# Weighing and summing of the 32 gathered cache lines, spread over the whole attention loop by the keys of its units

## The chip, the cores and the metric

One NeuronCore of a Trainium2 chip runs the whole step as one program. The metric is the device time of one execution in microseconds (us). Three runs of the kernel before gave 2342.09, 2346.89 and 2352.07 us; their median is 2346.89 us. The profiled execution, from which all durations below come, took 2347.29 us.

## What is computed

The reference is one layer of a decoder. A prompt of 1024 tokens and 8 decode samples (one token each, with a past of 4096 positions) pass an input projection, three-branch attention (compressed, selected, window) beside a diagonal state-space model, an output projection, cross-attention and a SwiGLU feed-forward net. The part that the change touches is the compressed branch of the 8 samples. Their past lies in pages of 128 rows; each block of 32 rows is weighed with a table and summed, then projected:

```
def compress_blocks(rows, cmp_pos, cmp_proj):
    B, N = rows.shape[:2]
    blk = rows.reshape(B, N // CMP_BLOCK, CMP_BLOCK, 2, N_KV, HEAD_DIM)
    summ = jnp.einsum('bnlcgd,cld->bncgd', blk, cmp_pos)
    return jnp.einsum('bncgd,cde->bncge', summ, cmp_proj)
```

A softmax over those 128 compressed blocks of each sample then ranks the blocks of 64 rows; 13 of them (and the first and last) are fetched for the selected branch.

## The kernel before, in words

Everything stands in one hand-ordered program for five engines: PE (TensorE), DVE (VectorE), ACT (ScalarE), POOL (GpSimd) and SP (SyncE). All work tiles of PE pass through four PSUM slots in one written order, `psum_plan` (L136): a tile opens its slot when the tile four places earlier has been read out.

**The attention loop** (386 to 861 us of the span) handles the prompt. `attention_units` (L81) lists 136 units: 8 query tiles of 128 rows, for each first one compressed unit for all heads, then for each of 8 heads a selected unit with 128(i+1) keys and a window unit with at most 640 keys. In iteration a, PE computes the scores SC of unit a, the transposes TR of unit a-2 and the product with the values PV of unit a-3. DVE adds the bias to the scores and takes the row maximum (L2202, L2206), later scales the product into the output (L2233 for each head unit). ACT computes the exponential between the two, and copies the transposes out of PSUM. So SC of a unit goes PE, DVE, ACT, back to PE for TR, ACT for the copy, PE for PV, DVE for the output, with two iterations of lead (`AHEAD`).

**The lines.** The past rows of the samples come by indirect gathers as 32 "lines" (4 for each sample, `n` = line, `k = n // 8` is the quarter of the block, `b = n % 8` the sample), each 128 partitions by 2048 numbers. POOL gathers line n+1 into a ring of three tiles (`past_line`, L1270, `gring`) once line n-2 has been summed, and loads the table `posB` of a new quarter when the last line of the old one is weighed (`weigh_line`, L1277). DVE works on a line in three parts, one part at the end of an iteration (`sum_lines`, L2076): part 0 weighs all 2048 numbers (L2084), part 1 adds 1024 numbers to 1024, part 2 adds 512, then 256, and in quarters 1 to 3 adds 256 more to the running sum `summ`. The first part stands in iteration `SUMS_AT` = 2, and from then on there is one in every iteration, so the 96 parts fill iterations 2 to 97:

```
SUMS_AT = 2
BETWEEN = {SUMS_AT + 3 * 4 * DB + 1 + 2 * b: [("sT", b), ("sP", b)] for b in range(DB)}
BETWEEN.update({122: ["sc"], 124: ["sps", "scT"], 127: ["sov", "ix1"], 130: ["ix2"]})
```

**What stands between.** `BETWEEN` (L96) inserts the rest of the samples' compressed branch behind iterations: for each sample PE transposes its sums (`sT`), waits until ACT has copied them to `sTm` (L1527), and multiplies them with the projection (`sP`, L826 to 831), in iterations 99, 101, ..., 113. In iteration 122 the scores `sc` follow, in 124 `sps` and `scT` (with the selection chain on DVE, three operations over 960 numbers among others), in 127 `sov` and `ix1`, in 130 `ix2`, which gives DVE the line numbers of the selected rows (L2139). `sTm` are two buffers at 4128 of the arena, which is the place of the second ring tile.

**Behind the loop.** POOL waits for the line numbers, issues three gathers of selected rows (`gather`, L1319), waits until the last scores have been read, and issues 24 loads of the window rows `nbuf` (L1338 to L1342) into the place of the bias table. SP streams weights (`glu_w`, then eight tiles of `xkv`) from the end of the scores on, ACT loads `mem_prompt`. PE runs the gated unit's tiles, the memory keys and values `mk`, and then the window rows `wT` and the selected rows `gT`.

Of the kernel before, what the change touches and what calls it, by code (L numbers as in the profile page):

```python
# [16 lines left out]
P = 128  # L17
# [4 lines left out]
DB = 8  # L22
# [58 lines left out]
def attention_units():  # L81

    out = []
    for i in range(NT):
        out.append((i, 0, 0, 0, 4 * (i + 1)))
        for h in range(NH):
            out.append((i, h, 1, 0, P * (i + 1)))
            k0 = max(0, i - 4) * P
            out.append((i, h, 2, k0, P * (i + 1) - k0))
    return out  # L90
# [1 line left out]

SUMS_AT = 2
BETWEEN = {SUMS_AT + 3 * 4 * DB + 1 + 2 * b: [("sT", b), ("sP", b)] for b in range(DB)}  # L96
BETWEEN.update({122: ["sc"], 124: ["sps", "scT"], 127: ["sov", "ix1"], 130: ["ix2"]})

def ffn_items():  # L100
# [88 lines left out]
def hymba_step(nc, x_prompt, x_sample, cache_kv_cmp, cache_kv_sel, cache_kv_win, state_ssm_re, state_ssm_im,  # L189
# [8 lines left out]
    with ctx:  # L198
# [8 lines left out]
        flip = sb("flip", [P, P])  # L207
# [14 lines left out]
        pblk = sb("pblk", [P, 2, P])  # L222
# [3 lines left out]
        apow = sb("apow", [P, 6, 2, NPAIR])  # L226
# [14 lines left out]
        def at(first, *shape):  # L241
            n = int(np.prod(shape))
            v = A[:, first:first + n]
            if len(shape) == 2:
                v = v.rearrange("p (a b) -> p a b", b=shape[1])
            elif len(shape) == 3:
                v = v.rearrange("p (a b c) -> p a b c", b=shape[1], c=shape[2])
            elif len(shape) == 4:
                v = v.rearrange("p (a b c d) -> p a b c d", b=shape[1], c=shape[2], d=shape[3])
            return v  # L250
# [38 lines left out]
        CP = at(37152, 2, NPAIR, 5, 32)  # L289
        Tm = [at(42272, P), at(43296, P)]  # L290
        Wm = [at(42400, 2, P), at(43424, 2, P)]
        sTm = [at(4128, 2, P), at(4384, 2, P)]
        posB = at(43872, ROWS, P)
        WT = at(44896, 2, NPAIR, P)

# [97 lines left out]
        def slot(key):  # L393
            s = U[key] % 4
            return PS[:, 2 * s:2 * s + 2, :].rearrange("p a b -> p (a b)")
# [11 lines left out]
        filled = sem("filled")  # L407
# [94 lines left out]
        def full(eng, key):  # L502

            eng.wait_ge(filled, U[key] + 1)
# [5 lines left out]
        def free(ins, key):  # L510

            ins.then_inc(emptied[U[key] % 4], 1)
# [128 lines left out]
        def _(pe):  # L641
# [8 lines left out]
            def mm(out, lhsT, rhs, start=True, stop=True):  # L650
                return nc.tensor.matmul(out, lhsT=lhsT, rhs=rhs, start=start, stop=stop, skip_group_check=True)  # L651
# [41 lines left out]
            s = open_("par")  # L693
# [27 lines left out]
            s = open_("C")  # L721
# [3 lines left out]
            s = open_("h0")  # L725
            for part in range(2):
                for j in range(NPAIR):
                    c = (part * NPAIR + j) * DB
# [22 lines left out]
            for j in range(NPAIR):  # L751
# [3 lines left out]
                s = open_(("SB", j))  # L755
# [8 lines left out]
            for i in range(NT + 1):  # L764
                c0, n = token_tile(i)
                s = open_(("kv", i))
# [8 lines left out]
            s = open_("cproj")  # L775
# [7 lines left out]
            for j in range(NPAIR):  # L783
                s = open_(("V", j))
# [4 lines left out]
                if j >= 8:  # L789
                    h = j - 8  # L790
                    pe.wait_ge(hank_in[h % 2], 16 * (h // 2 + 1))
                    s = open_(("bt", h))
# [4 lines left out]
            s = open_("ys")  # L797
# [7 lines left out]
            s = open_("st")  # L805
            tr(s[0:32, 0:P], H[:, NC].rearrange("p a j -> p (a j)")).then_inc(filled, 1)
            for q in range(4):
                s = open_(("sst", q))
# [6 lines left out]
            def compressed_branch(key):  # L815

                if key[0] == "sT":

                    b = key[1]
                    pe.wait_ge(summ_ready, b + 1)  # L820
                    s = open_(key)
                    for c in range(2):
                        ins = tr(s[:, c * P:(c + 1) * P], summ[:, b, c * P:(c + 1) * P])
                    ins.then_inc(filled, 1)
                elif key[0] == "sP":

                    b = key[1]
                    read_out(pe, ("sT", b))
                    s = open_(key)
                    mm(s[:, 0:P], pblk[:, 0], sTm[b % 2][:, 0])  # L830
                    mm(s[:, P:2 * P], sTm[b % 2][:, 1], pblk[:, 1]).then_inc(filled, 1)
                elif key == "sc":

                    read_out(pe, ("sP", DB - 1))
                    read_out(pe, ("sP", DB - 2))
                    pe.wait_ge(qz_ready, 1)
                    s = open_(key)
                    for b in range(DB):
                        ins = mm(s[0:64, 0:P], qz[:, b], kcTs[:, b], b == 0, b == DB - 1)
                    ins.then_inc(filled, 1)  # L840
                elif key == "sps":

                    pe.wait_ge(pc_ready, 1)
                    s = open_(key)
                    mm(s[0:64, 0:P], same[:, :], Pc[0:64]).then_inc(filled, 1)
                elif key == "scT":
                    s = open_(key)
                    tr(s[:, 0:64], Pc[0:64]).then_inc(filled, 1)
                elif key == "sov":
                    read_out(pe, "scT")  # L850
                    s = open_(key)
                    for b in range(DB):
                        ins = mm(s[:, b * 8:b * 8 + 8], vcs[:, b], PcT[:, b * 8:b * 8 + 8])
                    ins.then_inc(filled, 1)
                elif key == "ix1":

                    pe.wait_ge(phys_ready, 1)
                    s = open_(key)
                    tr(s[0:SLOTS, 0:64], phys[0:64, 0:SLOTS]).then_inc(filled, 1)
                elif key == "ix2":  # L860
                    read_out(pe, "ix1")
                    s = open_(key)
                    mm(s[0:SL, 0:64], spread[:, :], p15[0:SLOTS]).then_inc(filled, 1)
# [4 lines left out]
            for a in range(n_at + AHEAD + 1):  # L868
                if a < n_at:
                    i, h, br, k0, nk = AT[a]  # L870
                    lo = 64 * (h % 2)
                    s = open_(("SC", a))
# [510 lines left out]
        def _(act):  # L1383
# [3 lines left out]
            def f(out, in_, func=ACT.Copy, **kw):  # L1387
                return a_.activation(out, in_, func, **kw)  # L1388
# [132 lines left out]
            def compressed_branch(key):  # L1521
                if key[0] == "sT":
                    b = key[1]
                    full(act, key)
                    if b >= 2:
                        full(act, ("sP", b - 2))
                    free(f(sTm[b % 2].rearrange("p a c -> p (a c)"), slot(key)[:, 0:256]), key)  # L1527
                elif key[0] == "sP":
                    b = key[1]
                    full(act, key)  # L1530
                    own.step(f(kcTs[:, b], slot(key)[:, 0:P]))
                    free(f(vcs[:, b], slot(key)[:, P:2 * P]), key)
                elif key == "sps":
                    softmax_rows(1, pw_raw, pw_exp, Pc[0:64], 64)
                elif key == "scT":
                    full(act, key)
                    free(f(PcT, slot(key)[:, 0:64]), key)
                elif key == "sov":
                    full(act, key)
                    free(f(osT[:, 0], slot(key)[:, 0:64]), key)  # L1540
                elif key == "ix1":
                    full(act, key)
                    free(f(p15[0:SLOTS], slot(key)[0:SLOTS, 0:64]), key)
# [232 lines left out]
        def _(dve):  # L1776
# [299 lines left out]
            def sum_lines(n, part):  # L2076

                k, b = n // DB, n % DB
                flat = gring[n % 3]
                if part == 0:  # L2080
                    dve.wait_ge(gat[n % 3], 16 * (n // 3 + 1))
                    dve.wait_ge(posB_in, 32 * (k + 1))
                    r = flat.rearrange("p (r c g d) -> p (r c) g d", r=ROWS, c=2, g=2)
                    tt(r, r, posB.rearrange("p r (c d) -> p (r c) d", c=2).unsqueeze(2)  # L2084
                       .to_broadcast([P, 2 * ROWS, NKV, HD])).then_inc(weighted, 1)
                elif part == 1:
                    dve.wait_ge(weighted, n + 1)
                    own.step(tt(flat[:, 0:1024], flat[:, 0:1024], flat[:, 1024:2048], ALU.add))
                else:
                    own.settle()  # L2090
                    own.then(tt(flat[:, 0:512], flat[:, 0:512], flat[:, 512:1024], ALU.add))
                    if k == 0:
                        tt(summ[:, b], flat[:, 0:256], flat[:, 256:512], ALU.add).then_inc(gat_used, 1)
                    else:
                        own.then(tt(flat[:, 0:256], flat[:, 0:256], flat[:, 256:512], ALU.add))
                        tt(summ[:, b], summ[:, b], flat[:, 0:256], ALU.add).then_inc(gat_used, 1)
                    if k == 3:
                        dve.wait_ge(gat_used, n + 1)
                        dve.sem_inc(summ_ready, 1)
# [57 lines left out]
            for a in range(n_at + AHEAD + 1):  # L2157
# [76 lines left out]
                if t + 1 >= 0 and t + 1 < n_at:  # L2234
# [7 lines left out]
                    else:  # L2242
                        tt(st[:, 56 + rn:57 + rn], st[:, 48 + rn:49 + rn], gates[:, i, 3 * h + br:3 * h + br + 1])\
                            .then_inc(dve_gate, 1)
                if 0 <= a - SUMS_AT < 3 * 4 * DB:
                    sum_lines((a - SUMS_AT) // 3, (a - SUMS_AT) % 3)
                for key in BETWEEN.get(a, []):
                    compressed_branch(key)

# [266 lines left out]
```

## Time and profile before

| | |
|---|---|
| median of three runs | 2346.89 us |
| profiled execution | 2347.29 us |
| its span on the core | 2345.6 us |
| attention loop in it | 385.9 to about 861 us |
| busy PE / DVE / ACT over the span | 86% / 44% / 26% |
| granted TensorE clock, mean of the execution | 0.879 of full |

A time outside the span (2347.29 - 2345.6 = 1.7 us) is start and end of the program and is not touched. Busy shares are averages over stages with different limits, so the loop is read query tile by query tile.
### The profile page before, as it was taken

To read this page: it belongs to the slowest core of one execution; us is meant where nothing else is said; L and a number is where in the kernel's file an instruction comes from. 1 tells how busy PE (TensorE), PEld (TensorE's weight loads), DVE (VectorE), ACT (ScalarE), POOL (GpSimd) and SP (SyncE) were. 2 spreads that over 40 slices of the span, in tenths; PEclk is the share of its full clock that TensorE was granted. 3 is DMA by queue.
4 is the path that set the end of the run, shared out by engine and by line. 5 is a ranking of instruction groups with operands and counts; after the bars stand their busy time and mean duration, and the time that the engine had idled before them with its cause. 6 is when DMAs were issued, how large, how long until landed. Compare 5 with 4: busy or idle time off the path is not lost.

```text
span 2345.6 us, 28566 instructions
## 1 busy us (share of the span) xinstructions
PE 2026.3 (86%) x11440; PEld 1735.8 (74%) x11440; DVE 1038.6 (44%) x2439; ACT 609.3 (26%) x1228; POOL 140.3 (6%) x236
## 2 busy tenths in 40 slices
PE   7699997788888988676978899589999999999994
PEld 5465554577777877544975586489999999999993
DVE  6859725999884531005243031623232322323235
ACT  3031113334445441213232122521111111111112
POOL 2001112101100020200000100000000000000000
PEclk9899897557888899666998879789999999999997
DMA  5020003433310065730300301011111111111102
GB/s 127 20 73 32 32 0 119 143 118 121 114 55 1 1 160 179 167 88 10 118 28 27 135 1 36 28 39 52 37 55 37 52 48 48 52 37 55 37 19 81
DMA packets 122315, 151.19 MB, mean 64 GB/s; under 512 B 13256, under 2 KB 104560, under 8 KB 116136
## 3 DMA queue, kind: packets, MB, share of 16 engines
q0 software_dynamic: 17152, 80.63, 11.2%
q1 hardware_dynamic: 102600, 60.77, 9.0%
q10 hardware_dynamic: 2432, 7.96, 0.9%
q8 instruction: 92, 1.51, 0.3%
q14 instruction: 39, 0.32, 0.0%
HBM read 137.03 MB, written 12.31 MB: 64 GB/s over the span
## 4 chain that ended last, share of the span: by engine, by line
PE 48%; DVE 5%; issue 2%; DMA 1%; ACT 1%; POOL 0%; DVEq 0%; POOLq 0%
PE PS L651 46%; PE PS L655 2%; DVE A L2372 1%; DVE A L1781 1%; ACT A L1388 1%; DMA A<-in_cache_mem_kv 1%; DMA A<-new_selected_row 0%; DVE hL L1781 0%; DVE hRaw L1781 0%; DVE A L2383 0%; DVE A L2346 0%; DMA A<-in_norm_g 0%; DVE mA L1781 0%; DVE mS L2348 0%; DVE A L2324 0%
## 5 line engine op out<-in xcount | busy, mean ns | idle before, releaser
L651 PE MATMUL PS<-A 128*128 128x64 f32 (+15 forms) x3728 | 747.9, 361 | 35.5 <-ACT A L1388 28.0
L651 PEld LDWEIGHTS PS<-A 128*128 128x128 f32 (+4 forms) x3728 | 554.2, 206 | 227.2 <-issue 72.8
L655 PE MATMUL PS<-ident,A 128*128 128x128 f32 (+7 forms) x1528 | 277.3, 331 | 207.8 <-DVE A L2383 53.8
L655 PEld LDWEIGHTS PS<-ident,A 128*128 128x128 f32 (+7 forms) x1528 | 211.3, 166 | 257.9 <-issue 61.2
L1388 ACT ACTIVATE A<-PS 128x256 f32<-128x256 f32 (+17 forms) x404 | 229.0, 586 | 607.1 <-PE PS L651 487.0
L1781 DVE TENSOR_TENSOR A<-A 128x1024 f32<-128x1024 f32 (+12 forms) x397 | 304.6, 773 | 9.5 <-DMA A<-in_cmp_pos 0.3
L651 PE MATMUL PS<-hH,wL 128*128 128x344 f32 x1056 | 224.2, 321 | 2.9 <-issue 2.9
L651 PE MATMUL PS<-hL,wH 128*128 128x344 f32 x1056 | 224.3, 321 | 0.0
L651 PE MATMUL PS<-hH,wH 128*128 128x344 f32 x1056 | 223.7, 320 | 0.0
L651 PEld LDWEIGHTS PS<-hH,wL 128*128 128x128 f32 x1056 | 177.2, 189 | 4.1 <-issue 4.1
L651 PEld LDWEIGHTS PS<-hL,wH 128*128 128x128 f32 x1056 | 177.7, 189 | 0.0
L651 PEld LDWEIGHTS PS<-hH,wH 128*128 128x128 f32 x1056 | 177.3, 188 | 0.0
L1781 DVE TENSOR_TENSOR wL<-wRaw,wH 128x1024 fp32r<-128x1024 f32 (+2 forms) x76 | 82.1, 1082 | 208.1 <-ACT wH L1388 207.9
L1388 ACT ACTIVATE A<-A,st 128x640 f32<-128x640 f32 (+9 forms) x131 | 96.4, 736 | 248.5 <-DVE st L2206 225.1
L1388 ACT ACTIVATE wH<-wRaw 128x1024 fp32r<-128x1024 f32 (+2 forms) x76 | 71.6, 944 | 213.4 <-PE PS L651 213.4
L1781 DVE TENSOR_TENSOR A<-A,PS 128x688 f32<-128x688 f32 x112 | 72.4, 688 | 117.2 <-PE PS L651 113.9
L651 PE MATMUL PS<-gH,wL 128*128 128x344 f32 x528 | 114.2, 325 | 8.6 <-DVE A L1781 4.1
L651 PE MATMUL PS<-gL,wH 128*128 128x344 f32 x528 | 112.5, 321 | 0.0
L651 PE MATMUL PS<-gH,wH 128*128 128x344 f32 x528 | 112.2, 321 | 0.0
L1781 DVE TENSOR_TENSOR gRaw<-gRaw,PS 128x688 f32<-128x688 f32 (+1 forms) x44 | 28.5, 688 | 183.1 <-PE PS L651 183.1
L651 PE MATMUL PS<-kL,qS 128*128 128x512 f32 (+3 forms) x192 | 89.1, 464 | 12.3 <-DVE qS L1781 12.3
L651 PEld LDWEIGHTS PS<-gH,wL 128*128 128x128 f32 x528 | 87.6, 189 | 15.1 <-issue 15.1
(266 smaller groups left out, 1778.3 us busy)
## 6 DMA issues: line engine op xcount, KB each, us to landing
wRaw<-in_ffn_wi SPq DMA_DIRECT2D x44, 512.0 KB, 3.7
wRaw<-in_ffn_wo SPq DMA_DIRECT2D x28, 384.0 KB, 3.0
out<-A POOLq DMA_DIRECT2D x16, 512.0 KB, 3.2
A<-in_cache_mem_kv POOLq DMA_DIRECT2D x16, 512.0 KB, 5.3
A<-in_x_prompt SPq DMA_DIRECT2D x8, 512.0 KB, 8.1
A<-in_w_in SPq DMA_DIRECT2D x8, 512.0 KB, 10.6
A<-bias_by_distance POOLq DMA_DIRECT2D x8, 512.0 KB, 3.9
A<-in_xkv SPq DMA_DIRECT2D x8, 512.0 KB, 12.5
```

The source lines that it names most:

```text
L651: return nc.tensor.matmul(out, lhsT=lhsT, rhs=rhs, start=start, stop=stop, skip_group_check=True)
L655: return nc.tensor.transpose(out, in_, ident[b:b + n, b:b + n])
L1388: return a_.activation(out, in_, func, **kw)
L1781: return v.tensor_tensor(out, a, b, op)
L2372: free(v.scalar_tensor_tensor(dtmp[0:r, i % 2], slot(key)[0:r], st[0:r, 9 + i % 2:10 + i % 2], grow[0:r], ALU.mult, ALU.mult), key)
```

## The change

`line_starts` gives each unit a cost of 1000 plus its keys, and starts a line wherever 1/32 of the cost of units 2 to 125 has gone by (at least three iterations apart). Worked out, the starts are iterations 2, 8, 13, 18, 22, 27, 32, 36, 40, 45, 49, 53, 57, 61, 64, 68, 72, 76, 79, 83, 86, 90, 93, 97, 100, 104, 107, 110, 113, 117, 120 and 123; a line's three parts stand in three iterations in a row. `sT` and `sP` of a sample move to the iteration behind its last part: 103, 107, 110, 113, 116, 120, 123, 126. `sc` moves from 122 to 131, `sps` and `scT` from 124 to 133, `sov` and `ix1` from 127 to 135, `ix2` from 130 to 137. Since the ring is now in use while `sT` runs, `sTm` moves to `flip` and the first part of `apow` (both free by then), is one buffer for each half instead of two for both, and ACT copies it in two pieces.

```
-SUMS_AT = 2
-BETWEEN = {SUMS_AT + 3 * 4 * DB + 1 + 2 * b: [("sT", b), ("sP", b)] for b in range(DB)}
-BETWEEN.update({122: ["sc"], 124: ["sps", "scT"], 127: ["sov", "ix1"], 130: ["ix2"]})
+def line_starts():
+
+
+    cost = [1000 + nk for _, _, _, _, nk in attention_units()]
+    total, gone, starts = sum(cost[2:126]), 0, []
+    for a in range(2, 126):
+        if len(starts) < 4 * DB and gone >= total * len(starts) / (4 * DB) and (not starts or a >= starts[-1] + 3):
+            starts.append(a)
+        gone += cost[a]
+    return starts
+
+
+LINE_AT = line_starts()
+SUMS = {a + part: (n, part) for n, a in enumerate(LINE_AT) for part in range(3)}
+BETWEEN = {LINE_AT[3 * DB + b] + 3: [("sT", b), ("sP", b)] for b in range(DB)}
+BETWEEN.update({131: ["sc"], 133: ["sps", "scT"], 135: ["sov", "ix1"], 137: ["ix2"]})
...
-        sTm = [at(4128, 2, P), at(4384, 2, P)]
+        sTm = [flip[:, :], apow[:, 0:4].rearrange("p a b c -> p (a b c)")]
...
-                    mm(s[:, 0:P], pblk[:, 0], sTm[b % 2][:, 0])
-                    mm(s[:, P:2 * P], sTm[b % 2][:, 1], pblk[:, 1]).then_inc(filled, 1)
+                    mm(s[:, 0:P], pblk[:, 0], sTm[0])
+                    mm(s[:, P:2 * P], sTm[1], pblk[:, 1]).then_inc(filled, 1)
...
-                    if b >= 2:
-                        full(act, ("sP", b - 2))
-                    free(f(sTm[b % 2].rearrange("p a c -> p (a c)"), slot(key)[:, 0:256]), key)
+                    if b >= 1:
+                        full(act, ("sP", b - 1))
+                    own.step(f(sTm[0], slot(key)[:, 0:P]))
+                    free(f(sTm[1], slot(key)[:, P:2 * P]), key)
...
-                if 0 <= a - SUMS_AT < 3 * 4 * DB:
-                    sum_lines((a - SUMS_AT) // 3, (a - SUMS_AT) % 3)
+                if a in SUMS:
+                    sum_lines(*SUMS[a])
```

Counted by query tile (iterations 17i to 17i+16), the 96 parts stood 15, 17, 17, 17, 17, 13, 0, 0 before and stand 9, 11, 12, 13, 14, 15, 15, 7 after. Insertions of `sT` and `sP` stood 2 in tile 5 and 6 in tile 6, and stand 5 in tile 6 and 3 in tile 7.

## Rows read from the trace of the kernel before

**Rows 1.** The page's head: the span, and busy time of each engine.

```profile
span 2345.6 us, 28566 instructions
...
PE 2026.3 (86%) x11440; PEld 1735.8 (74%) x11440; DVE 1038.6 (44%) x2439; ACT 609.3 (26%) x1228; POOL 140.3 (6%) x236
```

**Rows 2.** Windows, one per query tile: length; busy PE, PEld, DVE, ACT, POOL; clock; DMA.

```profile
385.90:436.70 50.80, 27.44 (x115) 21.28 (x114) 34.44 (x122) 20.80 (x60) 10.48 (x19) 0.55 0.45 154
436.70:484.60 47.90, 38.53 (x163) 31.19 (x162) 42.88 (x141) 16.68 (x58) 7.71 (x8) 0.50 0.39 127
484.60:537.30 52.70, 46.25 (x211) 39.68 (x210) 46.98 (x149) 20.16 (x59) 6.89 (x8) 0.60 0.36 125
537.30:590.40 53.10, 43.38 (x259) 36.48 (x258) 49.34 (x143) 23.92 (x59) 5.43 (x6) 0.84 0.34 119
590.40:650.40 60.00, 51.50 (x339) 46.50 (x338) 53.32 (x158) 26.65 (x58) 7.71 (x8) 0.86 0.33 109
650.40:717.50 67.10, 59.51 (x378) 54.29 (x377) 51.05 (x161) 31.80 (x65) 1.92 (x2) 0.82 0.11 37
717.50:786.50 69.00, 59.64 (x428) 54.98 (x427) 30.15 (x128) 35.37 (x78) 0.00 (x0) 0.90 0.00 1
786.50:861.00 74.50, 69.56 (x503) 64.23 (x503) 39.82 (x169) 34.92 (x64) 11.56 (x20) 0.91 0.28 62
```

**Rows 3.** Waits of the stretch 406 to 650: total, times, longest.

```profile
ACT A L1388 <- DVE st L2206: 136.1, 76, 5.1
```

**Rows 4.** Groups by form, DVE, 386 to 720: the adds and weighing of the lines.

```profile
L1781 DVE TENSOR_TENSOR A<-A 128x2048 f32<-128x2048 f32 x32 | 73.1, 2285 | 0.3 <-DMA A<-in_cmp_pos 0.3
L1781 DVE TENSOR_TENSOR A<-A 128x1024 f32<-128x1024 f32 x32 | 39.0, 1219 | 0.0
...
L1781 DVE TENSOR_TENSOR A<-A 128x256 f32<-128x256 f32 x56 | 23.8, 425 | 1.9
L1781 DVE TENSOR_TENSOR A<-A 128x512 f32<-128x512 f32 x32 | 21.9, 685 | 0.0
```

**Rows 5.** Windows of L2233 alone (one for each head unit): length, busy DVE (count), clock.

```profile
651.30:700.70 49.40, 3.29 (x12) 0.83 0.13 44
777.80:796.20 18.40, 1.70 (x6) 1.00 0.00 1
723.50:777.80 54.30, 3.12 (x11) 0.87 0.00 1
800.40:842.50 42.10, 2.53 (x9) 0.84 0.04 10
842.60:855.70 13.10, 1.14 (x4) 1.00 0.99 210
```

**Rows 6.** Windows, all engines, of the first of those five stretches.

```profile
651.30:700.70 49.40, 43.18 (x273) 39.22 (x272) 42.02 (x124) 23.57 (x48) 1.92 (x2) 0.83 0.13 44
```

**Rows 7.** Windows, all engines, ten microseconds late in query tile 2.

```profile
526.00:536.00 10.00, 9.63 (x40) 8.33 (x40) 9.37 (x29) 4.16 (x13) 2.81 (x3) 0.50 0.46 147
```

**Rows 8.** Timeline around one insertion: start, length, engine, operation, idle before.

```profile
742.93 1.17 ACT L1388 ACTIVATE A<-PS 128x896 f32<-128x896 f32 x2
...
744.15 0.49 PE L651 MATMUL PS<-A,pblk 128*128 128x128 f32 x2 [1.39 <-ACT A L1388]
...
744.90 0.45 ACT L1388 ACTIVATE A<-PS 128x128 f32<-128x128 f32 x2 [0.80 <-PE PS L651]
```

**Rows 9.** Timeline of POOL: first selected gather, first load of the window rows.

```profile
839.00 1.00 POOL L1322 DMA_INDIRECT A<-in_cache_kv_sel,line  x1 [169.42 <-DVEq L2141]
...
854.15 0.57 POOL L1338 DMA_DIRECT2D A<-in_cache_kv_win  x1 [9.82 <-DVE st L2206]
```

**Rows 10.** Timeline of PE behind the loop: the one wait for weights.

```profile
901.79 16.18 PE L651 MATMUL PS<-A 128*128 128x128 f32 x128 [3.35 <-DMA A<-in_xkv]
```

**Rows 11.** Windows behind the loop, all engines, DMA share and GB/s last.

```profile
880.00:900.00 20.00, 17.08 (x141) 16.62 (x139) 8.55 (x24) 1.54 (x4) 4.25 (x8) 0.94 0.98 308
900.00:920.00 20.00, 18.21 (x148) 18.09 (x148) 0.00 (x0) 2.58 (x7) 0.00 (x0) 0.91 0.49 139
```

## The prediction

> **What bounds the kernel now.** The page comes first: the profiled execution has a span of 2345.6 us, and PE is busy for 86% of it [rows 1]. That share says little about one stage, so the next view is the windows, cut at the loop's eight query tiles. The whole loop is 475 us. In tile 0 DVE is busy 34.4 of 50.8 us; the loop only starts to run some 20 us into it. In tiles 1 to 4 DVE is busy 42.88 of 47.9, 46.98 of 52.7, 49.34 of 53.1 and 53.32 of 60.0 us, so 89 to 93%, while PE stands at 80 to 88%, mostly at a low granted clock (0.50, 0.60, 0.84, 0.86). In tile 6, which has no part of a line, DVE is busy 30.15 of 69.0 us [rows 2]. The waits say the same: from 406 to 650 us ACT stood 136.1 us, 76 times, for the scores' evacuation on DVE [rows 3]. So DVE paces tiles 1 to 4 and most of 5, and PE with its round trips over ACT paces 6 and 7. The change takes DVE work from the first group and gives it to the second.
>
> **What is moved.** By form, the weighing is 32 x 2285 ns, the first add 32 x 1219, the second 32 x 685 and the 256 adds 56 x 425: 73.1 + 39.0 + 21.9 + 23.8 = 157.8 us, over 96 parts 1.64 us each, and 1.54 in quarter 0, which has one add less [rows 4]. Nothing of it goes away. The parts by tile go from 15, 17, 17, 17, 17, 13, 0, 0 to 9, 11, 12, 13, 14, 15, 15, 7, so the question is what a part costs where it leaves and where it lands.
>
> **Where parts leave.** Tile 0 loses 6: at most 6 x 1.54 = 9.2 us. Its PE ran at a clock of 0.55 and there are short units without cover behind it, so I take -6 (ends -3 and -9.2). Tile 1 loses 6: DVE would need 9.9 us less, 38.0 us at the same idleness, but PE is busy 38.53 us at 0.50 [rows 2], so PE at its lower level stops it near 40.5: -7 (ends -5 and -9.9). Tile 2 loses 5, 8.2 us at most. Late in it PE at 0.50 is busy 9.63 of 10 us [rows 7], so at the lower level almost nothing could be gained, while at the tile's mean clock of 0.60 PE has 6.5 us of idle time: -7 (ends -1 and -8.2). Tile 3 loses 4: -6.5 (at most 6.6), as its clock of 0.84 leaves PE 9.7 us idle. Tile 4 loses 3: -4.5 (at most 4.9). For the clock of these tiles the rows show 0.50 while PE waited in every unit for DVE, and 0.84 to 0.86 from tile 3 on, where units are longer.
>
> The Trainium skill, page "TensorE: Matmul & The Clock Gate", section "What's actually happening", says that the throttled state is the default and that activity releases it. By that rule a PE that DVE holds up less would be granted its upper level sooner, and tiles 0 to 2 would give all of 9.2 + 9.9 + 8.2 us in place of 20, so 7 us more; no stretch of this trace shows tile 1 at the upper level.
>
> **Tiles 5 to 7.** The unit is the price here. L2233 runs once for each head unit. With a part in every iteration, 13 units of tile 5 (12 and a compressed one) took 49.4 us, 3.80 each; 6 units of tile 6 without part or insertion took 18.4 us, 3.07 each; 12 units of tile 6 (11 and a compressed one) with 6 insertions of sT and sP took 54.3 us, so an insertion costs (54.3 - 12 x 3.07) / 6 = 2.9 us; 9 units of tile 7 across sc, sps, sov, ix1 and ix2 took 42.1 us, and 4 bare ones 13.1 us, 3.27 each, so that chain costs 42.1 - 29.4 = 12.7 us [rows 5]. Check: 17 x 3.07 + 6 x 2.9 = 69.6 for tile 6, against 69.0 in the windows. In those 13 units DVE was busy 42.0 of 49.4 us [rows 6]; it is the bound there, with the usual gaps of its fences. A part in a late iteration therefore costs 3.80 - 3.07 = 0.73 us, not 1.64: the rest runs while DVE would wait for PE. Its ends are 0 (all covered) and 1.64 (nothing covered).
>
> An insertion costs because sT needs an ACT copy that stands behind an exponential and a long copy in ACT's order: PE idles before sP, and SC of the next unit is queued behind it, with DVE and then ACT waiting for that [rows 8]. After the change five of the eight insertions (107, 110, 113, 120, 123) share their iteration with a part 0, whose 2.29 us run on DVE meanwhile. I take 2.3 us for each (ends 0.6, that is 2.9 - 2.29, and 2.9). The extra copy piece on ACT is cheap: two 128x128 copies together take 0.45 us [rows 8], so at most 0.2 x 8 = 1.6 us, inside these ends. The single buffer's wait for the sP before it is for one at least three iterations old: nothing. The new operands (flip, apow) are read like the old ones: nothing.
>
> Tile 5: 15 x 3.80 + 2 x 3.07 = 63.1, before 67.1: -4. Tile 6: 63.1 + 5 x 2.3 = 74.6, before 69.0: +5.6. Tile 7: 7 parts x 0.73 = 5.1, 3 insertions x 2.3 = 6.9, and the chain from sc to ix2 now lies in the last eight iterations, three of which have no scores, so some of its 12.7 us falls together with the emptying of the pipeline: -2 (ends 0 and -6). Together +10.
>
> **Queues moved past.** POOL's gathers of lines follow the sums by themselves; it waits for DVE before each of them, so they merely come later. The line numbers of the selected rows were ready at 839, 22 us before the loop's end, and the window rows' loads began at 854.2 [rows 9]. Now ix2 stands in the last iteration but one. The three gathers (120 rows of 8 KB each, 2.95 MB; 1 us each on POOL, and a small load behind each) start with the loop's end at 861, so the 24 loads begin near 866 in place of 854, 12 us later. PE reads the window rows only after mk, which ends at 918 [rows 10], so nobody waits for those directly. But the DMA engines stood at a share of 0.98 and 308 GB/s from 880 to 900 and at 0.49 after that [rows 11], while the xkv weights came in, and PE waited once for them, 3.35 us [rows 10]. 2.95 MB at 308 GB/s are 9.6 us of traffic more in that stretch. With half of the next 20 us free I take +3 (ends -4, since mem_prompt and the first weights meet fewer window rows, and +9.6).
>
> **The sum.** Leaving: -6 -7 -7 -6.5 -4.5 -4 = -35. Arriving: +5.6 + 10 + 3 = +18.6. Net -16.4: 2347.3 - 16.4 = 2331 us. The profiled execution stands 0.4 us over the median of the runs, so the forecast for the median is the same, 0.7% faster. Its own range is 2322 to 2342. A measurement of this kernel can tell about 0.5% (12 us) from no change: below 2335 is faster, above 2359 slower.
>
> **The rivals.**
> A, chance 0.20: late parts are covered. In tile 6 DVE idles 39 of 69 us [rows 2], and two iterations of lead could absorb a part. Then tiles 6 and 7 change only by the insertions, -2.9 + 8.7 - 2 = +3.8, and the sum is -35 + 3.8 + 3 = -28: 2319, and 2312 with the 7 us of the early clock. The rule of the clock gate named above is part of this case. Against it: the 3.80 us units of tile 5 exist.
> B, chance 0.26: no difference. Either tiles 1 and 2 stay at the lower level and PE stops them early (-22 in place of -35), or DMA traffic behind the loop costs its 9.6 us and an insertion its full 2.9 us (8 x 0.6 more). The first gives -22 + 18.6 = -3, the second -16.4 + 6.6 + 4.8 = -5: about 2343. For it: PE at 0.50 was 96% busy in places.
> C, chance 0.06: slower. The mechanism is the order on DVE: a part stands between the output of one unit and the evacuation of the next scores, and SC of the unit after waits for the slot. If PE meets that gap in each late iteration, a part costs its full 1.64 us: tile 6 becomes 69.0 + 15 x 1.64 - 2.9 = 90.7 (+21.7), tile 7 +7 x 1.64 + 8.7 = +20.2, together +41.9 and with 9.6 behind the loop +51.5 against -35: +16, 2364. It decides from the price p of a late part: with full insertions and +3 behind the loop the sum is -35 - 2.9 + 8.7 + 3 + 22p, which is zero at p = 1.2 us. Against it: 13 units of tile 5 show 3.80, not 3.07 + 1.64 = 4.71.
> That the change doesn't move what it says can be left out: the starts follow from the code.
>
> **How the numbers follow.** Forecast 0.48, A 0.20, B 0.26, C 0.06. Of the forecast's own share 0.42 lies below 2335. Faster 0.42 + 0.20 = 0.62, same 0.06 + 0.26 = 0.32, slower 0.06. The range takes in the forecast's ends, most of A and of B: 2314 to 2350.
>
> **What would show it.** Windows of the changed kernel by query tile: DVE's load near 0.9 in tiles 2 to 6; lengths near 45, 41, 46, 46.5, 55.5, 63, 74.5 and 84.5 us. Tile 6 longer than 69 us confirms the price of late parts; 66 or less speaks for A, 85 or more for C. PE's clock in tiles 1 and 2: over 0.7 means that the early clock rose. The gap of PE before each sP shows the insertions. PE's wait for xkv behind the loop should lie between 3 and 10 us. The prediction is wrong if tiles 0 to 4 give less than 20 us together, or tiles 6 and 7 take more than 30.

## The result, and the profile after

The changed kernel took 2363.05 us (median of four runs, 2362.05 to 2371.06) against 2347.47 us before: a ratio of 1.008, with a 95% interval of 1.0053 to 1.0107. The forecast was 2331 us with a range of 2314 to 2350. The kernel became slower by 16 us, 0.8%, where 0.7% faster was forecast.

The profiled execution is the slowest of the four, 2371.06 us, so 8 us over their median; a second profiled execution of the same kernel took 2364.11 us. Where the two differ, both are given. The page's head, which answers to [rows 1]:

```profile
span 2369.3 us, 28575 instructions
...
PE 2051.2 (87%) x11440; PEld 1762.1 (74%) x11440; DVE 1038.1 (44%) x2439; ACT 609.0 (26%) x1236; POOL 139.9 (6%) x236
```

The windows of the changed kernel by query tile answer to [rows 2] (length; busy PE, PEld, DVE, ACT, POOL; granted clock; DMA share; GB/s):

```profile
383.60:430.70 47.10, 25.72 (x115) 20.90 (x114) 27.25 (x116) 20.65 (x60) 8.55 (x17) 0.54 0.36 122
430.70:472.90 42.20, 37.26 (x163) 31.39 (x162) 31.92 (x127) 16.55 (x58) 3.73 (x4) 0.50 0.30 100
472.90:519.90 47.00, 43.60 (x209) 37.71 (x208) 39.07 (x134) 20.15 (x58) 5.77 (x6) 0.61 0.32 102
519.90:573.50 53.60, 45.90 (x259) 39.21 (x258) 44.90 (x144) 23.55 (x58) 4.14 (x5) 0.77 0.23 79
573.50:629.60 56.10, 49.07 (x339) 44.92 (x338) 47.50 (x151) 27.00 (x58) 6.27 (x7) 0.88 0.32 104
629.60:699.30 69.70, 60.84 (x368) 56.21 (x367) 52.35 (x159) 29.40 (x59) 6.63 (x7) 0.78 0.25 84
699.30:777.60 78.30, 65.19 (x422) 59.70 (x421) 52.56 (x152) 34.30 (x78) 4.85 (x5) 0.83 0.20 68
777.60:877.50 99.90, 87.54 (x520) 79.67 (x520) 52.27 (x188) 38.60 (x78) 1.57 (x2) 0.75 0.06 17
```

DVE carries what the change says: 42.88 us of tile 1 became 31.92, and the 30.15 of tile 6 became 52.56. Lengths in us; the last column is the span less the end of the loop, which is read here at 860.7 for the kernel before ([rows 2] cut it at 861.0):

| | tile 0 | 1 | 2 | 3 | 4 | 5 | 6 | 7 | behind the loop |
|---|---|---|---|---|---|---|---|---|---|
| before | 50.8 | 47.9 | 52.7 | 53.1 | 60.0 | 67.1 | 69.0 | 74.2 | 1484.9 |
| after, first profile | 47.1 | 42.2 | 47.0 | 53.6 | 56.1 | 69.7 | 78.3 | 99.9 | 1491.8 |
| after, second profile | 46.2 | 42.2 | 48.8 | 53.9 | 56.6 | 63.7 | 75.7 | 96.4 | 1492.2 |
| mean change | -4.2 | -5.7 | -4.8 | +0.6 | -3.7 | -0.4 | +8.0 | +23.9 | +7.1 |
| forecast | -6 | -7 | -7 | -6.5 | -4.5 | -4 | +5.6 | +10 | +3 |

So three things went wrong at once: tiles 0 to 4 gave 18 us in place of 31 (and tile 5 nothing in place of 4), tile 7 took 24 in place of 10, and the stretch behind the loop 7 in place of 3. The timeline of the changed kernel shows what happens at the end of tile 7 (start, length, engine, operation, idle time before it):

```profile
851.92 1.15 DVE L1795 TENSOR_TENSOR A<-A,jota 64x960 f32<-64x960 f32 x1
...
853.19 1.15 DVE L1795 TENSOR_TENSOR A<-A 64x960 f32<-64x960 f32 x1
...
854.38 1.15 DVE L2150 TENSOR_REDUCE A<-A 64x15 f32<-64x960 f32 x1
...
856.87 1.30 PE L668 MATMUL PS<-ident,A 128*128 128x128 f32 x5 [3.33 <-DVE st L2220]
...
859.05 6.97 PE L664 MATMUL PS<-A 128*128 128x64 f32 x32 [0.88 <-ACT A L1401]
...
875.81 0.99 POOL L1335 DMA_INDIRECT A<-in_cache_kv_sel,line  x1 [108.03 <-DVEq L2155]
```

The three operations over 960 numbers hold DVE while the scores of the last unit but one wait for it; PE waits 3.33 us for their evacuation. By then no further scores are left for PE to work on in the meantime. The windows before and after that wait:

```profile
838.30:856.70 18.40, 13.83 (x104) 12.24 (x103) 11.51 (x48) 5.27 (x12) 0.00 (x0) 0.97 0.10 30
856.70:875.80 19.10, 18.05 (x83) 17.33 (x83) 3.25 (x22) 5.70 (x10) 0.00 (x0) 0.50 0.19 55
```

PE ran at a granted clock of 0.97 before the wait and at 0.50, its lower level, for 19 us after it, 18.05 of them busy, with the 16 small products of `sov` (8 columns each) and the last transposes and products of the loop. The first gather is issued at 875.8, with the loop's end at 877.5.

The second profile shows that this one wait is not the whole story. There PE has no such wait, but it is at its lower level already 8 us earlier, counted from the end of the loop, behind a wait of 1.00 us for the samples' softmax:

```profile
841.58 0.69 PE L664 MATMUL PS<-A,same 64*64 64x128 f32 x2 [1.00 <-DVE A L2088]
```

The same two products took 0.43 us in the first profile. Yet from the start of `sc` to the end of the loop the two executions took nearly the same: 38.0 us (839.50 to 877.5) and 38.3 us (831.92 to 870.2). Behind the loop PE waits for the norm of `mem_prompt` (6.86 us, 4.42 before) and twice for weights of `xkv` (once, 3.35 us, in [rows 10]):

```profile
899.23 3.67 PE L668 MATMUL PS<-ident,A 128*128 128x128 f32 x16 [6.86 <-DVE A L2269]
...
920.56 16.04 PE L664 MATMUL PS<-A 128*128 128x128 f32 x128 [5.33 <-DMA A<-in_xkv]
937.59 3.84 PE L664 MATMUL PS<-A 128*128 128x128 f32 x32 [0.98 <-DMA A<-in_xkv]
```

### The profile page after: what moved, and what is told of

Same layout as the page of the kernel before. It is cut to its first block, busy times and chain, and to the rows that moved or that the text cites. A ratio compares the mean times of both kernels' runs of the same rounds, so it can differ in the third digit from the quotient of the medians.

```text
span 2369.3 us, 28575 instructions
## 1 busy us (share of the span) xinstructions
PE 2051.2 (87%) x11440; PEld 1762.1 (74%) x11440; DVE 1038.1 (44%) x2439; ACT 609.0 (26%) x1236; POOL 139.9 (6%) x236
## 4 chain that ended last, share of the span: by engine, by line
PE 47%; DVE 5%; issue 2%; DMA 1%; ACT 1%; POOL 0%; DVEq 0%; POOLq 0%; ACTq 0%
PE PS L664 45%; PE PS L668 2%; DVE A L2386 1%; DVE A L1795 1%; ACT A L1401 1%; DMA A<-in_cache_mem_kv 1%; DMA A<-new_selected_row 1%; DVE hL L1795 0%; DVE hRaw L1795 0%; DVE A L2360 0%; DVE A L2397 0%; DVE mA L1795 0%; DMA A<-in_norm_g 0%; DVE mS L2362 0%; DVE A L2338 0%
## 5 line engine op out<-in xcount | busy, mean ns | idle before, releaser
L664 PE MATMUL PS<-A 128*128 128x64 f32 (+15 forms) x3728 | 760.7, 366 | 37.6 <-ACT A L1401 27.1
L664 PEld LDWEIGHTS PS<-A 128*128 128x128 f32 (+4 forms) x3728 | 568.2, 211 | 226.8 <-issue 72.0
L668 PE MATMUL PS<-ident,A 128*128 128x128 f32 (+8 forms) x1528 | 288.5, 341 | 201.4 <-DVE A L2397 50.2
L668 PEld LDWEIGHTS PS<-ident,A 128*128 128x128 f32 (+8 forms) x1528 | 221.4, 172 | 251.9 <-issue 56.7
L1401 ACT ACTIVATE A<-PS 128x1024 f32<-128x1024 f32 (+16 forms) x396 | 226.4, 590 | 612.0 <-PE PS L664 491.2
L1401 ACT ACTIVATE A<-A,st 128x640 f32<-128x640 f32 (+9 forms) x131 | 96.4, 736 | 260.6 <-DVE st L2220 236.7
```

The lines of the kernel that those rows point to most:

```text
L668: return nc.tensor.transpose(out, in_, ident[b:b + n, b:b + n])
```

## The experiments

They ran in three groups, each beside the kernel before on one chip; its median in the groups was 2346.8, 2345.9 and 2347.1 us. Times of different groups, such as the changed kernel (2363.05 and 2362.7) and most of its variants, are therefore comparable to about 1 us on top of their own scatter. Theory 1, formed from the profile above: the parts of the lines are about neutral, and it is the tail (sc to ix2 in the last eight iterations) that costs. The rival: parts in the late iterations cost it.

**The changed kernel again.**

> The changed kernel once more, for a second profile of it. Its first profile was 8 us above its other runs. If the stretches at the lower clock level in query tiles 3 and 5 are a feature of the schedule, both tiles come out as before (53.6 and 69.7 us, within 1 us); if they are chance, they differ by several us. Time: 2363.

2362.7 us (ratio 1.006, 1.0043 to 1.0077). Tile 5 took 63.7 us at a clock of 0.84, against 69.7 at 0.78; tile 3 stayed at 53.9. So 6 us of the first profile's 8 were chance in tile 5, and tile 3's missing gain is a feature of the schedule. Later runs bear it out: tiles 0 to 4 have the program of the kernel before in four other runs below and that of the changed kernel in three, so there are five profiles of each. The means of tiles 0 to 4 are 50.6, 47.8, 53.1, 53.3 and 58.7 us before and 46.4, 41.9, 47.3, 53.1 and 56.8 us after, 263.4 and 245.5 together: 18 us, and nothing in tile 3.

**Only insertions and tail late.**

```
-LINE_AT = line_starts()
+LINE_AT = [2 + 3 * n for n in range(4 * DB)]
```

with the positions of `BETWEEN` written out as in the change.

> The lines' parts stand in iterations 2 to 97 as in the kernel before; only sT and sP (103 to 126) and sc to ix2 (131 to 137) stand where the change puts them, and sTm too. Theory 1, that the late chain is what costs (PE waits for DVE's selection chain with no scores left to cover it, falls to the lower clock, and the gathers start with the loop's end): 12 to 20 us slower than before, 2359 to 2367. Rival, that the parts in the late iterations are what costs: 0 to 5 us over before, at most 2352.

2360.9 us, 1.0059 (1.0039 to 1.0079): 14 us slower, with not one part moved, as theory 1 has it. The changed kernel is only 2 us slower than this run, which the scatter of both covers: spreading the parts came out about neutral. The profiled execution is the fastest of the four, 2352.8 us, 8 us under their median, so its windows show less than the usual time. Tiles 6 and 7:

```profile
707.30:769.70 62.40, 54.74 (x422) 50.26 (x421) 30.46 (x131) 35.63 (x81) 0.00 (x0) 0.97 0.00 1
769.70:859.30 89.60, 81.79 (x520) 74.82 (x520) 39.62 (x169) 37.00 (x75) 1.58 (x2) 0.80 0.07 19
```

**Only the tail late.**

```
-BETWEEN.update({122: ["sc"], 124: ["sps", "scT"], 127: ["sov", "ix1"], 130: ["ix2"]})
+BETWEEN.update({131: ["sc"], 133: ["sps", "scT"], 135: ["sov", "ix1"], 137: ["ix2"]})
```

> The kernel before with nothing changed but the places of sc, sps and scT, sov and ix1, ix2: 131, 133, 135, 137 in place of 122, 124, 127, 130. The insertions stay at 99 to 113. Theory 1 (this tail is what costs, not the places of the insertions): 10 to 15 us slower than before, of which about 7 in query tile 7 and 7 behind the loop. Rival (the three insertions among the units of tile 7, or their meeting with the tail, cost it): within 5 us of before.

2360.5 us, 1.0056 (1.0032 to 1.008). This one line of the change costs 15 us; the two intervals don't part it from the whole change. Tiles 6 and 7:

```profile
716.40:786.30 69.90, 61.39 (x426) 56.58 (x425) 30.13 (x128) 35.27 (x78) 0.00 (x0) 0.88 0.00 1
786.30:866.80 80.50, 72.33 (x502) 66.85 (x502) 39.54 (x169) 34.94 (x64) 1.57 (x2) 0.88 0.08 21
```

Tile 7 is 6.3 us longer than before; behind the loop stand 1495.2 us (2362.0 - 866.8) in place of 1484.9, so 10.3 more (7.1 in the changed kernel; what makes the 3 us between them is open). Where the 6.3 come from shows when both tiles are cut at the first scores of the last selected unit but one, here and in the kernel before:

```profile
830.65 0.50 PE L651 MATMUL PS<-kL,qS 128*128 128x512 f32 x1
```

```profile
842.00 0.48 PE L651 MATMUL PS<-kL,qS 128*128 128x512 f32 x1
```

Up to there the tile takes 44.4 us in place of 55.5: moving the chain away gave 11.1. From there to the end of the loop it takes 36.2 us (830.65 to 866.8) in place of 18.7 (842.00 to 860.7): landing it at the end cost 17.5. Before, PE was at its upper level in that stretch (1.00 from 838.3 to 860.7); here it is at 0.55 from 845.0 to 866.8, behind a wait of 3.33 us like the one above. How the 17.5 us divide between waits and the lower level was not separated.

**Window rows first.** On POOL the three gathers go behind the 24 loads, in the changed kernel:

```
-            pool.wait_ge(line_ready, 1)
-            pool.wait_ge(gat_used, 4 * DB)
-            for n in range(3):
-                gather(n)
...
                 pool.dma_start(nbuf[P - 1:P, b, 3], win_row[b:b + 1]).then_inc(nbuf_in, 16)
+            pool.wait_ge(line_ready, 1)
+            pool.wait_ge(gat_used, 4 * DB)
+            for n in range(3):
+                gather(n)
```

> The changed kernel with POOL issuing the 24 loads of the window rows before it waits for the line numbers and issues the first three selected gathers. The stretch behind the loop was 7 us longer than before. If POOL's order, which starts the window rows 12 us later, is the cause, 5 to 7 us faster than the changed kernel. If the 2.95 MB of gathers in that stretch are the cause whatever the order, within 3 us of it.

2358.2 us, 1.0048 (1.0028 to 1.0068), 4.5 us under the changed kernel by the medians, though the ten times lie between 2347.9 and 2367.6 and the interval overlaps the changed kernel's. The profile is clearer than the times: behind the loop stand 2356.9 - 871.5 = 1485.4 us, as before the change, and the waits for `xkv` are gone:

```profile
892.75 3.68 PE L668 MATMUL PS<-ident,A 128*128 128x128 f32 x16 [6.24 <-DVE A L2268]
897.79 30.31 PE L664 MATMUL PS<-A 128*128 128x128 f32 x256 [1.36 <-issue]
```

The whole of `mk` (256 products) now runs in one piece of 30.3 us. The wait for the norm stays (6.24 us). The loads of the window rows now start at 852.8 and are all issued by 864.8, before the loop's end at 871.5; in the changed kernel they start at 881.1, behind its end at 877.5. The 2.95 MB of gathers start at the loop's end in both. So by these profiles, one against two, it was the order on POOL, which pushed the window rows among the weights, and not the gathers' own traffic, that cost 6 to 7 us.

**sP one iteration behind sT, before the change and after it.**

```
-BETWEEN = {LINE_AT[3 * DB + b] + 3: [("sT", b), ("sP", b)] for b in range(DB)}
+BETWEEN = {LINE_AT[3 * DB + b] + 3: [("sT", b)] for b in range(DB)}
+BETWEEN.update({LINE_AT[3 * DB + b] + 4: [("sP", b)] for b in range(DB)})
```

and the same in the kernel before, at 99 + 2b and 100 + 2b.

> The kernel before with sP one iteration behind its sT (sT in 99, 101, ..., 113, sP in 100, 102, ..., 114). Theory 1: an insertion costs 2.9 us because PE waits for ACT's copy of sT in the same iteration; with an iteration between, most of 8 x 2.9 = 23 us goes: 12 to 20 us faster, 2327 to 2335. Rival: ACT's copy stands behind the exponential in either case and the wait only moves to the next tile in that PSUM slot: within 4 us of before.

2335.2 us, 0.9955 (0.9935 to 0.9974). Tile 6 falls from 69.0 to 58.0 us and holds the upper level throughout:

```profile
708.60:766.60 58.00, 53.12 (x430) 49.83 (x429) 30.33 (x131) 35.52 (x80) 0.00 (x0) 1.00 0.00 1
766.60:842.60 76.00, 70.24 (x502) 64.70 (x502) 39.44 (x168) 34.97 (x64) 11.20 (x20) 0.89 0.27 61
```

> The changed kernel with each sP one iteration behind its sT. In the kernel before the same edit gave 11.6 us. If an insertion among late parts stalls in the same way, 10 to 16 us faster than the changed kernel, 2347 to 2353. If the parts on DVE had covered most of the stall already, as the prediction took it in part, at most 5 us.

2348.5 us, 1.0019 (0.9996 to 1.0041), so 14 us under the changed kernel. Tiles 6 and 7, which were 77 and 98 us in the mean of the two profiles:

```profile
693.40:761.50 68.10, 59.81 (x422) 54.77 (x421) 53.59 (x159) 34.82 (x79) 4.85 (x5) 0.90 0.24 83
761.50:853.10 91.60, 82.75 (x520) 75.05 (x520) 50.70 (x182) 37.51 (x78) 1.57 (x2) 0.81 0.06 18
```

The same edit gave 12 us before the change and 14 after it, alike within the scatter: late parts don't cover an insertion's stall. PE's waits for the copy of sT (total, times, longest) in tile 6 of the changed kernel are:

```profile
PE PS L664 <- ACT apow L1401: 10.1, 5, 3.0
```

and in tile 6 of the kernel with only the insertions and the tail late:

```profile
PE PS L664 <- ACT apow L1401: 5.9, 5, 1.9
```

Both have the same five insertions there. In the changed kernel each follows an iteration that ends with a part 2 on DVE, which could delay the next scores, ACT's exponential and, behind it, the copy PE waits for. That is not shown: in the next run four of the five insertions follow a lightened part, and the same waits still come to 9.6 us, against 10.1 here and 8.4 in the second profile of the changed kernel. A part 2 keeps its adds of 256 there, 0.85 us of 1.5, so the reading isn't refuted either; what makes the waits longer stays open.

**The late parts made light.** Lines 25 to 31 (iterations 104 to 125), with `few = n >= 25`:

```
+                    m = 1 if few else 2 * ROWS
+                    r = flat.rearrange("p (r c g d) -> p (r c) g d", r=ROWS, c=2, g=2)[:, 0:m]
...
+                    m = 16 if few else 1024
...
+                    m = 16 if few else 512
```

> The changed kernel, with the parts of the last seven lines (iterations 104 to 125) worked on few columns: part 0 on 128 of 2048, part 1 on 16 of 1024, part 2's first add on 16 of 512. Most of the weighing and summing of these lines is left out, some 24 us of DVE work. Prediction's price (0.73 of 1.64 us for a late part): 10 to 12 us faster than the changed kernel. Rival C (a late part costs all its time): 22 to 26 us faster. Rival A (covered): within 4 us.

2353.7 us, 1.0034 (1.0012 to 1.0055), 9 us under the changed kernel. Tiles 6 and 7:

```profile
696.10:771.60 75.50, 64.95 (x422) 60.38 (x421) 38.97 (x163) 35.56 (x81) 4.86 (x5) 0.82 0.21 73
771.60:866.00 94.40, 82.69 (x520) 76.11 (x520) 42.82 (x183) 37.74 (x77) 1.58 (x2) 0.79 0.06 18
```

DVE's load in these tiles fell by 23.0 us (52.56 + 52.27 to 38.97 + 42.82), so a us of late DVE work costs 9.2 / 23.0 = 0.40 us (9.2 from 2362.9, the mean of the changed kernel's two medians). The prediction had 0.73 / 1.64 = 0.45. The ten times of this run lie between 2345.5 and 2366.6 us, so by an estimate from that scatter the 9.2 are 3 to 13 and the price 0.1 to 0.6. That is under rival C's full price, and in accord with the prediction's; it hardly parts the prediction from rival A, which allowed 4 us.

**All parts made light, before and after the change.** The same edit for every line. The first run has the program of the kernel before with the light parts, the second that of the changed kernel.

> The kernel before with every part worked on few columns (part 0 on 128 of 2048, part 1 on 16 of 1024, part 2's first add on 16 of 512), so most of the weighing and summing is left out: about 110 us of DVE work less. It gives the floor of query tiles 0 to 5 without parts. The prediction has DVE as the bound of tiles 1 to 4 and PE at its lower level close under it in tiles 1 and 2: then tiles 1 and 2 stop near 40 us each, and tiles 3 and 4 fall to 40 and 50. Rival: tile 3 stays near 50 us, so what the change took from it could give nothing.

2282.1 us, 0.9703 (0.9663 to 0.9743). Tiles 0 to 5 of the first, the floor under the parts:

```profile
380.30:419.70 39.40, 24.68 (x115) 20.75 (x114) 18.15 (x124) 21.51 (x63) 10.49 (x19) 0.56 0.54 182
419.70:456.90 37.20, 36.12 (x163) 31.52 (x162) 23.84 (x140) 16.98 (x58) 7.63 (x8) 0.50 0.55 180
456.90:496.80 39.90, 33.26 (x211) 28.75 (x210) 27.19 (x144) 19.51 (x57) 7.38 (x8) 0.84 0.50 167
496.80:540.60 43.80, 39.11 (x258) 33.85 (x258) 29.17 (x142) 23.98 (x61) 4.91 (x6) 0.88 0.43 145
540.60:591.60 51.00, 47.18 (x337) 43.18 (x336) 34.51 (x160) 27.01 (x59) 7.69 (x8) 0.90 0.40 128
591.60:650.00 58.40, 53.74 (x380) 49.78 (x379) 35.13 (x158) 30.17 (x63) 1.91 (x2) 0.88 0.12 43
```

Tiles 1 to 4 fall to 37.2, 39.9, 43.8 and 51.0 us, about where the expectation had them (40, 40, 40 and 50), and tile 3 doesn't stay near 50. But the price of a us of DVE work is far from 1: 53.2 us for 94.1 us of work in tiles 0 to 4 together, 0.57, and in tile 3 alone 9.3 for 20.2, 0.46.

> The changed kernel with every part worked on the same few columns. If the late chain, and not the parts, is what makes the changed kernel slow, it stays 12 to 20 us behind the same edit of the kernel before. If the late parts are the cause, the two come out within 5 us of each other.

2291.2 us, 0.9755 (0.9719 to 0.9792), so 9 us behind, between the two expectations. Its tiles 1, 3 and 5:

```profile
423.90:457.30 33.40, 32.38 (x161) 29.35 (x160) 21.06 (x128) 17.08 (x61) 3.43 (x4) 0.55 0.37 126
...
494.90:536.00 41.10, 36.20 (x259) 30.60 (x258) 28.64 (x139) 22.43 (x57) 4.39 (x5) 0.96 0.31 104
...
581.50:632.20 50.70, 46.05 (x369) 42.34 (x367) 34.26 (x156) 29.14 (x59) 6.63 (x7) 1.00 0.33 108
```

Both edits take 111 us of DVE work away (1038.6 to 927.8 us busy over the span, and 1038.1 to 927.1). Before the change that gives 65 us, after it 72: 0.59 and 0.65 us of time for each us of DVE work. Spread over the loop, the parts cost in total no less than packed at its start, by the medians.

**Lines spread over a shorter stretch.** `range(2, 112)` in place of `range(2, 126)`, tail at 122 to 130 as before.

> The lines spread in proportion to the keys, but over iterations 2 to 112, sT and sP in 95... no: in 92, 95, ..., 113, and sc to ix2 at 122 to 130 as before. Parts by query tile 10, 13, 14, 15, 16, 17, 11, 0. Theory 1 (the late chain costs, the parts are worth about 1 us each where they leave and cost 0.73 us where they land): 0 to 8 us faster than before, about 2343. Rival (late parts cost their full 1.64 us): 15 parts land for 15 that leave, so 3 to 8 us slower.

2349.3 us, 1.0017 (1.0002 to 1.0032). 2.5 us slower than before: theory 1's 0 to 8 us faster is missed, and the rival's 3 to 8 us slower is met but for half a us. The rival's price, the full time of a late part, isn't shown by that, since the light late parts gave less. Tiles 0 to 2 gave what they give in the changed kernel (46.1, 41.9, 47.1 us), and tiles 5 and 6 took it back (77.0 and 74.4).

**Distance for every round trip, without and with the shorter spread.** The second half of the edit beyond sP:

```
+for _a, _keys in {119: ['sc'], 120: ['sx'], 121: ['sy'], 122: ['sps', 'scT'], 123: ['s1'], 124: ['s2', 'sov'], 125: ['s3'], 127: ['ix1'], 129: ['ix2']}.items():
+    BETWEEN.setdefault(_a, []).extend(_keys)
```

where `sx` is the exponential on ACT, `sy` the division on DVE, and `s1` to `s3` the three operations over 960 numbers.

> The kernel before with every round trip of the samples' branch given an iteration of its own: sP one behind sT; scores in 119, exponential on ACT in 120, the division on DVE in 121, sps and scT in 122, the three operations over 960 numbers in 123, 124 and 125, sov in 124, ix1 in 127, ix2 in 129. The 12.7 us that sc to ix2 cost are waits of PE for these round trips. If giving them distance takes the waits away, 18 to 24 us faster than before (11.6 for the insertions, the rest here): 2322 to 2328. If only the insertions give, 2335.

2331.2 us, 0.992 (0.9894 to 0.9946): the fastest run that does all the work, 16 us under the kernel before. It falls between the two expectations (2322 to 2328, and 2335), and its interval overlaps that of the split insertions alone. The profiled execution is its slowest, 2340.1 us. Tiles 6 and 7:

```profile
721.60:779.60 58.00, 53.11 (x430) 49.83 (x429) 30.32 (x131) 35.49 (x79) 0.00 (x0) 1.00 0.00 1
779.60:848.90 69.30, 66.22 (x502) 61.17 (x502) 39.07 (x169) 34.88 (x64) 11.23 (x20) 0.95 0.31 70
```

Tile 7 lost 5 us against 74.2 before, and 7 against 76.0 with only the insertions split. So of the 12.7 us that the expectation called waits, distance took away about half.

> The same round trips with distance, and the lines spread in proportion to the keys over iterations 2 to 112 in place of 2 to 97. Without the stalls of the insertions, PE keeps its upper level in tiles 5 and 6, and the parts that left tiles 0 to 2 show: 5 to 12 us faster than the kernel with the parts in 2 to 97, about 2316. Rival: what tiles 0 to 2 give is taken back in tiles 5 and 6, within 3 us of it.

2335.8 us, 0.9943 (0.9917 to 0.9968): 4.7 us slower than without the spread by the medians, within the scatter of both. The 5 to 12 us of gain didn't come; the rival's 3 us are passed a little, to the slow side. Tiles 5 and 6:

```profile
638.50:708.10 69.60, 61.38 (x387) 56.86 (x385) 55.44 (x164) 31.27 (x70) 7.70 (x8) 0.80 0.27 89
708.10:782.10 74.00, 65.66 (x419) 60.51 (x419) 49.05 (x152) 35.80 (x81) 0.94 (x1) 0.82 0.09 29
```

Tile 6 is 16 us longer than without the spread (58.0), at a clock of 0.82 in place of 1.00, for 11 parts and 18.7 us more of DVE work; tiles 0 to 2 gave 14.7 us (151.8 to 137.1 us together).

## Why the prediction was wrong

**What bounds the kernel now.** "DVE paces tiles 1 to 4" was half right. The busy share of 89 to 93% was read as a bound. With 65 us for 111 us of work, DVE was close to the bound but not alone on the path: 0.59 us of time for each us of its work.

**Where parts leave.** This is the first step that failed. The 24 parts that left tiles 0 to 4 took 36.3 us of DVE work with them (227.0 to 190.6 us busy), and the prediction credited -6 -7 -7 -6.5 -4.5 = -31 for them, 0.85 for each us. The two profiles show -17.8, so 0.49. A part was priced at nearly its full time where it left and at 0.45 of it where it landed; the runs show about half at either end, and with one price a move gives nothing. The changed kernel stands 2 us from the run with the parts left in place (2362.9 and 2360.9), and the spread to 112, with the tail in its old place, 2.5 us over the kernel before. The prediction had the ceiling of each tile in its own rows: [rows 5] gave 0.45 for the same work in tile 5, and nothing but the busy share said that tiles 1 to 4 were different. For tiles 0 to 2 the lower clock was named as the stop and -20 in total taken; -14.7 came. The largest miss is tile 3, -6.5 forecast: it gave nothing (+0.6) at a clock of 0.77 and 0.78 in place of 0.84, with 4.4 us less on DVE. With all parts light the same tile gave 9.3 us for 20.2, so it can give, but the first 4.4 us bought nothing. The clock alone doesn't explain it: in another profile of the same stretch, that of the changed kernel with split insertions, it was 0.84 again, and the tile still took 53.2 us. Why stays open. Tile 5 gave 0.4 in place of 4, and its five profiles run from 62.7 to 69.7 us.

**Tiles 5 to 7.** The price of a landing part isn't contradicted by the times (0.40, from 0.1 to 0.6, against 0.45), but single tiles show more: tile 6 with 15 parts took 77.0 us against 62.4 with none and the same insertions, for 22.7 us of DVE work, 0.64, and the spread to 112 with split insertions 16 us for 18.7. The insertion at 2.3 us was too cheap: three of them among tile 7's units, without parts, made it 89.6 in place of 80.5 us, 3.0 each, just over the upper end of 2.9. The idea that a part 0 in the same iteration would cover the stall was wrong: PE's waiting at an insertion was 1.2 us without parts and 2.0 with them (1.7 in the second profile).

**The tail.** The second step that failed, and the costliest: "-2 (ends 0 and -6)". It assumed that waits fall together with the emptying of the pipeline. The run with the tail alone late shows +6.3 in tile 7, outside both ends. The chain's price where it left was about right, 11.1 us against 12.7; where it landed it was 17.5 in place of the 10.7 that the sum assumes. The waits of sc to ix2 are followed by scores of later units before the change; at the end there are hardly any, and PE falls to its lower level, which the sum did not hold at all. Tile 7 as a whole can be followed from run to run: 74.2 before, 80.5 with the tail late, 89.6 with three insertions too, 98.1 with seven parts too. The steps of 6.3, 9.1 and 8.5 add up to the 23.9 by construction, and each rests on one or two profiles.

**Queues moved past.** The mechanism was named: gathers first, window rows 12 us later, PE waiting for `xkv`. The term was mis-sized, +3 in place of 7, which lies under its upper end of 9.6 (10.3 with the tail alone late). The window rows began 27 us later (881.1 in place of 854.2) and not 12, and the price was put on the gathers' traffic, where by the profile it was the window rows that met the weights.

**The rivals.** A (parts covered) is made unlikely by the 9 us that light late parts gave and by tile 6. C said slower, and slower it was, by 16 us, which is near C's 2364 by luck and not by C's mechanism: with the tail alone late and no part moved, about 15 of the 16 us are there. Of B the sizes came true, a gain of 18 where the parts left (it had 22), insertions at 3.0 us, 7 us behind the loop, all together where it took them one by one; but its reason was tiles 1 and 2 stopped early, and these missed by 3.5 us, tiles 3 and 5 by 10.7. What no rival held was that the tail itself costs 15 us. The conditions that it named for being wrong ("if tiles 0 to 4 give less than 20 us together, or tiles 6 and 7 take more than 30") came out on both counts: 17.8 and 31.9.

On the rule of the Trainium skill's page "TensorE: Matmul & The Clock Gate", section "What's actually happening": the tail agrees with it in the fall, 0.97 before the wait and 0.50 behind it, but not in what follows: PE was busy 18.05 of the next 19.1 us, and that activity didn't release the lower level. The hope drawn from it, that PE would rise to its upper level sooner in tiles 0 to 2, was not met: 0.54, 0.50 and 0.61 after against 0.55, 0.50 and 0.60 before, although PE was less held up. Even with hardly any part left, tile 1 stayed at 0.50 with PE busy 36.12 of 37.2 us.

## What to carry to other kernels

A busy share of 90% is not a marginal price: before moving work from a "bound" stage to a slack one, take the price of a unit of it from a pair of stretches on each side, by the same measure, or shrink it in place and time that. When a chain of round trips hangs on the moved work, price the chain's new place first: its waits need later work of the other engines to cover them, and there is hardly any at the end of a loop. Here cheap distance (one iteration between a transpose and the product that needs its copy) gave 12 us, and the balancing nothing.

## What the runs showed of the hardware

The same instructions in the same order took different times from one execution to the next, along with the granted clock. Tile 4 has the same program in five of these kernels: it took 60.0 us at 0.86 (before), 57.2 at 1.00, 57.3 at 1.00, 60.1 at 0.86 and 59.1 at 0.86. So a single profile tells a tile's length to some 3 us, and tile 5's to 7 (62.7 to 69.7 us over five profiles of the changed kernel's program there). PE at its lower level could be busy 18.05 of 19.1 us and stay there, and could be busy 97% of tile 1 at 0.50; in the same kernel tile 2 was granted 0.84.
